# A transformer block pair in float32 on one core: two tiles of the residual left to GpSimd in three norms, silu(c) computed in pieces, and an opening that shares each tile between two blocks

## The reference

```python
def rmsnorm_2(x, g):
    xf = x.astype(jnp.float32)
    y = xf * lax.rsqrt(jnp.mean(xf * xf, axis=-1, keepdims=True) + NORM_EPS)
    return (y * g.astype(jnp.float32)).astype(x.dtype)
...
    c_act = jax.nn.silu(c)
...
        mod = c_act @ ada_w[l] + ada_b[l]
        sh_m, sc_m, g_m, sh_f, sc_f, g_f = jnp.split(mod, 6, axis=-1)
        h = modulate(rmsnorm_2(x, norm_g[l, 0]), sh_m, sc_m)
        ...
        x = x + g_m[:, None, :] * rmsnorm_2(y, norm_g[l, 1])
        h = modulate(rmsnorm_2(x, norm_g[l, 2]), sh_f, sc_f)
        y = squared_relu_mlp(h, mlp_up_w[l], mlp_down_w[l])
        x = x + g_f[:, None, :] * rmsnorm_2(y, norm_g[l, 3])
```

## Time and profile before

| what | value |
|---|---|
| time, median of 3 runs | 1792.23 us |
| lowest and highest | 1791.45 and 1792.46 us |
| the profiled execution's own time | 1791.45 us |
| its span, first to last instruction | 1789.7 us |
| TensorE busy | 1746.8 us |
| VectorE busy | 1094.8 us |
| ScalarE busy | 632.2 us |
| GpSimd busy | 95.0 us |
| mean granted TensorE clock (1 is full) | 0.993 |

### The profile page before, as it was taken

The page is one execution under the profiler, slowest core; times in us unless marked ns, Lnnn a source line. Parts: engine busy times, 40 slices in busy tenths (PEclk is TensorE's granted clock), DMA queues, the critical chain, the costliest instruction groups (busy, mean ns, idle before and its releaser), DMA issues. The chain is left out here.

```text
span 1789.7 us, 22632 instructions
## 1 busy us (share of the span) xinstructions
PE 1746.8 (98%) x8124; PEld 1413.5 (79%) x8124; DVE 1094.8 (61%) x1603; ACT 632.2 (35%) x987; POOL 95.0 (5%) x155
## 2 busy tenths in 40 slices
PE   8989999999999999999999999999999999999996
PEld 7857677888888888887888888877767788888886
DVE  6676554655555576878656565667775865434354
ACT  4226444322222353244423142425444442323231
POOL 0000000000000000100100000010000100000001
PEclk9999999999999999999999999999999999999998
DMA  6421111444444434652245555521321234333221
GB/s 230 116 85 36 48 48 56 155 148 164 146 153 153 141 106 130 219 192 83 83 176 188 203 180 203 174 85 53 118 71 38 81 97 163 105 94 95 94 82 47
DMA packets 61951, 216.63 MB, mean 121 GB/s; under 512 B 7216, under 2 KB 9392, under 8 KB 61680
## 3 DMA queue, kind: packets, MB, share of 16 engines
q1 hardware_dynamic: 45072, 154.95, 25.7%
q0 software_dynamic: 16656, 60.04, 10.9%
q10 hardware_dynamic: 144, 0.59, 0.1%
HBM read 212.67 MB, written 2.10 MB: 120 GB/s over the span
## 5 line engine op out<-in xcount | busy, mean ns | idle before, releaser
L794 ACT ACTIVATE w_hi<-w_raw 128x1024 fp32r<-128x1024 f32 x284 | 299.0, 1054 | 409.0 <-PE psum L1952 372.1
L1950 PE MATMUL psum<-h_hi,w_hi 128*128 128x512 f32 x1080 | 421.4, 390 | 2.9 <-DVE h_lo L1200 2.9
L1952 PE MATMUL psum<-h_hi,w_lo 128*128 128x512 f32 x1080 | 420.2, 389 | 0.0
L1951 PE MATMUL psum<-h_lo,w_hi 128*128 128x512 f32 x1080 | 420.2, 389 | 0.0
L1175 DVE TENSOR_TENSOR w_lo<-w_raw,w_hi 128x1024 fp32r<-128x1024 f32 x284 | 347.2, 1223 | 116.6 <-ACT w_hi L794 108.7
L1950 PE MATMUL psum<-hid_hi,w_hi 128*128 128x512 f32 x736 | 286.3, 389 | 0.0
L1951 PE MATMUL psum<-hid_lo,w_hi 128*128 128x512 f32 x736 | 286.3, 389 | 0.0
L1952 PE MATMUL psum<-hid_hi,w_lo 128*128 128x512 f32 x736 | 286.3, 389 | 0.0
L1950 PEld LDWEIGHTS psum<-h_hi,w_hi 128*128 128x128 f32 x1080 | 202.7, 188 | 46.9 <-DVE h_lo L1200 3.8
L1951 PEld LDWEIGHTS psum<-h_lo,w_hi 128*128 128x128 f32 x1080 | 202.8, 188 | 42.3 <-issue 0.5
L1952 PEld LDWEIGHTS psum<-h_hi,w_lo 128*128 128x128 f32 x1080 | 202.7, 188 | 42.2
(11 more groups left out here) (342 smaller groups left out, 1964.5 us busy)
## 6 DMA issues: line engine op xcount, KB each, us to landing
w_raw<-in_wstream SPq DMA_DIRECT2D x284, 512.0 KB, 3.6
ada_raw<-in_ada POOLq DMA_DIRECT2D x112, 512.0 KB, 3.8
x<-in_xT SPq DMA_DIRECT2D x8, 256.0 KB, 5.1
outT<-x SPq DMA_DIRECT2D x16, 128.0 KB, 1.8
con<-in_consts SPq DMA_DIRECT2D x1, 1028.0 KB, 10.1
con<-in_rope ACTq DMA_DIRECT2D x1, 576.0 KB, 5.7
w_raw<-in_wstream SPq DMA_DIRECT2D x2, 256.0 KB, 3.7
c_row<-in_crow POOLq DMA_DIRECT2D x1, 512.0 KB, 4.0
```

Of the source, the lines that this page charges most:

```text
L794: act.activation(w_hi[:, slot, :], w_raw[:, slot, :], ACT.Copy).then_inc(whi_done, 1)
L1950: pe.matmul(bank, w_hi[:, slot, w], hi[:, ra + k, :], start=k == 0, stop=False)
L1951: pe.matmul(bank, w_hi[:, slot, w], lo[:, ra + k, :], start=False, stop=False)
L1952: mm = pe.matmul(bank, w_lo[:, slot, w], hi[:, ra + k, :], start=False, stop=k == nk - 1)
```

## The change

Four edits.

1. **Opening.** Blocks 0 and 1 share each k (`kouter=2`); their first halves are loaded behind tile 0, their second halves behind tile 3, block 2 behind tile 7. 18 warm calls instead of 15.
2. **silu(c)** is done in four quarters, behind the evacuations of the gemm of five blocks; the exp stands in that gemm too.
3. **All three norms** are now of the kind with gathered sums: the `close` norm becomes inst 1, the former inst 1 becomes inst 2. `NEW_WARM` is 27 instead of 18.
4. **Tiles 6 and 7** of x: ScalarE puts the gain into y in the gemm; GpSimd multiplies by rstd and adds to x, in the stage `resum`. VectorE's `new_step` is left for tiles 0 to 5. Several steps of `resummed` read or write PSUM instead of SBUF.

```diff
-WARM_START, WARM = 15, 9
+WARM_START, WARM = 18, 9
-NEW_WARM = 18
+NEW_WARM = 27
...
-    gemm("scaled", 3, "h", h, dst="proj", dst_at=0, qscale=True)
+    gemm("scaled", 3, "h", h, dst="proj", dst_at=0, qscale=True, kouter=2)
...
-    gemm("scaled", 5, "h", h, dst="proj", dst_at=3, qscale=True)
+    gemm("scaled", 5, "h", h, dst="proj", dst_at=3, qscale=True, silu=True)
...
-    mlp(h, (0, 8, 8, 7), (8, 8, 8, 0), "g_kv", "g_m1", "r_m1")
-    close("r_f0", 21, 16, keep=True)
-    hkv = norm("hid", gain="g_kv", shift=48, splits={7: 0})
+    mlp(h, (0, 8, 8, 7), (8, 8, 8, 0), "g_kv", "g_m1", "r_m1", fore=1, old="r_f0")
+    hkv = renew("r_f0", "g_kv", 48, 1, dst="hid")
...
+        OWN = DT - 2
...
+        def root_wide(inst):
+            return psum[:, O_BANK if inst == 1 else PT_BANK, :]
...
-                if c < 2:
-                    half = slice(c * S, (c + 1) * S)
-                    sp.dma_start(w_raw[:, 0, half], wstream[0][:, half]).then_inc(raw_loaded[0] if c else raw_half, 16)
-                if c in OPEN_W:
-                    n = OPEN_W.index(c) + 1
-                    sp.dma_start(w_raw[:, n, :], wstream[n]).then_inc(raw_loaded[n], 16)
+                if c in (0, 3):
+                    half = slice(0, S) if c == 0 else slice(S, D)
+                    for n in range(2):
+                        sp.dma_start(w_raw[:, n, half], wstream[n][:, half]).then_inc(raw_loaded[n] if c else raw_half[n], 16)
+                if c == DT - 1:
+                    sp.dma_start(w_raw[:, 2, :], wstream[2]).then_inc(raw_loaded[2], 16)
...
+                if s["kind"] == "resum":
+                    pool.wait_ge(rstd_done, s["at"]["rstd"])
+                    for c in (OWN, OWN + 1):
+                        pool.wait_ge(gained_done, 2 * s["inst"] + c - OWN + 1)
+                        pool.tensor_tensor(y[:, c, :], y[:, c, :], rstd[:, :], ALU.mult).then_inc(gained_mul, 1)
+                    for c in (OWN, OWN + 1):
+                        pool.wait_ge(gained_mul, 2 * s["inst"] + c - OWN + 1)
+                        pool.tensor_tensor(x[:, c, :], x[:, c, :], y[:, c, :], ALU.add).then_inc(x_pool, 1)
...
+                    if s.get("silu") and t.b == 0:
+                        act.wait_ge(ss_done, at_["ss"])
+                        act.wait_ge(c_loaded, 16)
+                        act.activation(c_exp, c_row[:, :], ACT.Exp, scale=-1.0).then_inc(c_step, 1)
...
+                        if c >= OWN:
+                            act.wait_ge(mul_done, DT * inst + c + 1)
+                            act.activation(y[:, c, :], y[:, c, :], ACT.Copy, scale=gain_of(s["old"], c)).then_inc(gained_done, 1)
...
+                    if s["second_of"] == 2:
+                        act.wait_ge(gained_mul, 2 * s["second_of"])
+                        act.activation(rstd[:, :], resum, ACT.Exp, scale=-0.5).then_inc(root_kept, 1)
...
+            def silu_c(i):
+
+                part = slice(i * D // 4, (i + 1) * D // 4)
+                dve.wait_ge(c_step, 2 * i + 1)
+                dve.tensor_scalar(c_exp[:, part], c_exp[:, part], 1.0, None, ALU.add).then_inc(c_step, 1)
+                dve.wait_ge(c_step, 2 * i + 2)
+                dve.reciprocal(c_exp[:, part], c_exp[:, part]).then_inc(c_step, 1)
+                dve.wait_ge(c_step, 2 * i + 3)
+                dve.tensor_tensor(c_row[:, part], c_row[:, part], c_exp[:, part], ALU.mult).then_inc(c_done, 1)
...
+                        if s.get("silu") and t.b >= 1:
+                            silu_c(t.b - 1)
...
-                dve.tensor_scalar(resum, resum, 0.0, None, ALU.max).then_inc(resum_done, 1)
-                dve.wait_ge(root_done, inst + 1)
+                dve.tensor_scalar(x_mean[:, :], resum, 0.0, None, ALU.max).then_inc(resum_done, 1)
                 new_step(s, 0)
-                dve.wait_ge(held_done, DT * inst + 1)
-                dve.tensor_tensor(x[:, 0, :], x[:, 0, :], y[:, 0, :], ALU.add).then_inc(x_done, 1)
+                dve.wait_ge(held_done, OWN * inst + 1)
+                dve.tensor_tensor(x[:, 0, :], x[:, 0, :], new_val(inst, 1), ALU.add).then_inc(x_done, 1)
...
-                for c in range(DT - 2):
+                for c in range(OWN - 2):
                     val(c)
                     new_step(s, c + 2)
                     low(c)
-                val(DT - 2)
-                val(DT - 1)
-                low(DT - 2)
+                val(OWN - 2)
+                for c in range(OWN - 1, DT):
+                    val(c)
+                    low(c - 1)
                 low(DT - 1)
+                if s["inst"] == 1:
+                    dve.wait_ge(root_kept, 1)
```

More of the change, by code:

```diff
@@ L151, in renew @@
         r0 = counts["rhs"]
-        add("renew", dict(val=DT, hi=DT, rhs=DT, xup=1, xpool=DT - 1), inst=inst, old=old, gain=name, shift=shift)
+        add("renew", dict(val=DT, hi=DT, rhs=DT, xup=1, xpool=DT - 1), inst=inst, old=old, gain=name, shift=shift, dst=dst)
         return r0
-    def close(gain, middle, end, keep=False):
-        total()
-        warm(middle)
-        rstd(EPS2, wide=True)
-        update(gain)
-        warm(end)
-        rstd(EPS2, keep=keep)
     def values(group, at):
@@ L251, in make_plan, with mlp @@
     h = renew("r_m0", "g_f0", 24, 0)
-    def mlp(h, up, down, *names, ends=0):
+    def mlp(h, up, down, *names, ends=0, **last):
         for g in range(4):
@@ L289, in make_plan @@
     take("g_f1")
-    gemm("acc", 8, "h", mix, dst="y", first=True, sq=True, fore=1, old="r_m1", kouter=2, begun=6,
+    gemm("acc", 8, "h", mix, dst="y", first=True, sq=True, fore=2, old="r_m1", kouter=2, begun=6,
          turn=-counts["o"] % BANKS)
-    h = renew("r_m1", "g_f1", 88, 1)
+    h = renew("r_m1", "g_f1", 88, 2)
     hid = mlp(h, (0, 0, 0, 0), (8, 0, 0, 0), "r_f1", ends=ENDS)
@@ L307 @@
 TURN = dict(diff=2, fox=1)
-OPEN_W = (4, 7)
 SUM_AT = 6
@@ L1179, in weighted @@
             def weighted(first, upto):
+                if first == 0:
+                    dve.wait_ge(c_done, 4)
                 for u in range(first, upto):
@@ L1332, in step @@
                         dve.wait_ge(out_done, t.o + 1)
-                        dve.tensor_copy(y[:, c, :], bank).then_inc(bank_free, 1)
+                        if s["first"]:
+                            dve.tensor_copy(y[:, c, :], bank).then_inc(bank_free, 1)
+                        else:
+                            dve.tensor_tensor(y[:, c, :], y[:, c, :], bank, ALU.add).then_inc(bank_free, 1)
                         dve.wait_ge(bank_free, BANKS + t.o + 1)
@@ L1465, in new_step @@
             def new_step(s, c):
-                dve.scalar_tensor_tensor(out=y[:, c, :], in0=y[:, c, :], scalar=gain_of(s["old"], c), in1=root_wide,
+                out = y[:, c, :] if c else new_val(s["inst"], 1)
+                dve.scalar_tensor_tensor(out=out, in0=y[:, c, :], scalar=gain_of(s["old"], c), in1=root_wide(s["inst"]),
                                          op0=ALU.mult, op1=ALU.mult).then_inc(held_done, 1)
@@ L1497, in renew @@
                 at_ = s["at"]
+                hi_out, lo_out = operand(s["dst"])
                 def val(c):
@@ L1502, in val @@
                     else:
-                        dve.wait_ge(x_pool, at_["xpool"] + c)
+                        dve.wait_ge(x_pool, at_["xpool"] + (c + 2 if c < OWN else c - OWN + 1))
                     if c >= 2:
                         dve.wait_ge(rhs_ready, at_["rhs"] + c - 1)
-                    dve.scalar_tensor_tensor(out=new_val(c), in0=x[:, c, :], scalar=gain_of(s["gain"], c), in1=root_new,
+                    dve.scalar_tensor_tensor(out=new_val(s["inst"], c), in0=x[:, c, :], scalar=gain_of(s["gain"], c),
+                                             in1=root_new(s["inst"]),
                                              op0=ALU.mult, op1=ALU.mult).then_inc(val_done, 1)
@@ L1827, in _ @@
                     split_lo(s["at"]["n"] + AHEAD, (s["at"]["n"] + AHEAD) % SPLIT)
-                    if s["group"] == 1 and s["slot"] == 2:
-                        silu_c()
                     if s["slot"] == 3:
@@ L1934, in step @@
                     slot = t.n0 % SPLIT
-                    halves = at_["n"] == 0 and isinstance(t.b, int) and t.b == 0
-                    if halves:
-                        pe.wait_ge(wlo_half, 1)
-                    else:
-                        pe.wait_ge(wlo_done, t.n + 1)
+                    pe.wait_ge(wlo_done, t.n + 1)
                     for q in range(s["nout"]):
@@ L1944, in step @@
                         for k in range(nk):
-                            if halves and k == nk // 2:
-                                pe.wait_ge(wlo_done, 1)
                             if t.j == 0 and q == 0:
@@ L1969, in gemm @@
                           .then_inc(aux_done, 1)
+                    if opening and k == nk // 2:
+                        pe.wait_ge(wlo_done, len(blocks))
                     outer(s, blocks, k)
@@ L2289, in _ @@
```

(4 more changed lines are left out.)

103 lines of the change are left out of this document (54 added, 49 removed).

## The result

The changed kernel takes 1778.41 us (median of 4 runs, 1777.44 to 1779.83) against 1791.9 before: ratio 0.9925, 95% interval 0.9908 to 0.9942. The forecast was 1777.6. The profiled execution took 1778.59, its span is 1776.8, against 1789.7: 12.9 us less. Totals of one kernel scatter by 2 to 4 us from one execution to the next, so the terms are read from stages.

The account below looks back on a forecast made before the run. TensorE, busy 98% of the span, bounds the kernel. Opening 2.5, silu 8.0, norm 0 0.5, norm 1 3.2 and norm 2 0.4 sum to 14.6 us: 1776.85 for the profiled execution, median 1777.6, range 1773.5 to 1781.5.

Parts of the forecast that it names:

- Opening: First gemm: TensorE starts at about 7.55 and ends three blocks at 24.1 against 26.64, 2.5 us earlier (1.0 to 3.1).
- silu: Before the attention pairs: idle time falls from 7.4 to 0.85, 6.6 us, plus 1.4 of clock; 8.0 (6.6 to 8.4).
- The clamp: In each norm, VectorE's clamp of the mean waits for the rest of GpSimd's third operation, costing 0.75 us.
- Rival B: No collision: the clamp runs beside GpSimd, 2.2 us more gained, 1775.4; chance 0.20.
- ScalarE's copy: In the norms, the added 0.6 us copy for c=7 ends about when TensorE's sum of y squared does: costs nothing.
- Norm 0: Tiles set the pace up to k=4, then TensorE; three blocks end at 864.8 against 865.25, 0.5 us better.
- Norm 1: First tile 5.35 us earlier, part given back by slower tiles; VectorE starts the second norm at 1223.35, not 1226.42: 3.2 gained.
- Norm 2: Idle time 2.1 us with no clock fall expected; end at 1439.4 against 1439.81, 0.4 us better.
- Rival C: The clock falls in norms 0 and 2 in spite of the filler: 2.2 us less gained, 1779.8; chance 0.17.
- D: In front of the pairs another wait takes silu's place, 5 of the 8 us gone: 1782.6; chance 0.04.
- E: Little change: the opening gains nothing and silu's pieces push the weights, 1788.6 to 1795.8; chance 0.03.
- F: Norms slower: GpSimd keeps VectorE off SBUF altogether, 11.6 us a norm, 1812; chance 0.03.

Follow-up runs that it names:

- g11: The changed kernel itself, profiled and measured once more: 1778.27 us, ratio 0.9927 to the kernel before.
- f6: Changed kernel with GpSimd's add of tile 6 held until VectorE's clamp is done and tile 7's behind tiles 1 to 5: 1776.59 us, ratio 0.9917.
- e2: Kernel before with the opening edit alone: 1789.8 us, ratio 0.999.
- e3: Kernel before with the two norm edits alone (GpSimd tiles, norm 1 from gathered sums, longer filler): 1788.54 us, ratio 0.9984.
- g10: Kernel before with only the filler of its two resummed norms lengthened, 58 and 66 matmuls for 36 each: 1790.52 us, ratio 0.9994.
- f7: Changed kernel with the 20 narrow matmuls of the forget gate's sums moved behind the next block of values: 1779.63 us, ratio 0.993.
- f8: Changed kernel with f6's and f7's edits, ScalarE's copy of tile 7 behind the root's copy, fillers of 56, 62 and 62 matmuls: 1774.71 us, ratio 0.9908.
- e4: Changed kernel without its GpSimd tiles, VectorE making the steps of tiles 6 and 7 itself: 1777.17 us, ratio 0.9917.
- e1: Kernel before with the silu edit alone: 1784.88 us, ratio 0.996.
- f5: Changed kernel with the filler lengthened by each norm's idle time, 64, 70 and 74 matmuls for 54 each: 1777.09 us, ratio 0.9923.
- g9: f8 with the narrow matmuls left together as in the changed kernel: 1775.39 us, ratio 0.9911.

## Why the prediction was right, and where it wasn't

The forecast was 14.6 us in sum; the medians have 13.5 and, beside g11, 14.1. In the profiled pair it is 12.9, and the 1.7 between are 0.8 of the opening and 1.5 of norm 2, less 0.6 that silu gave on top; norms 0 and 1 came out at the size forecast. That the median came within 0.8 of 1777.6 is in part luck: the misses have different signs.

**Opening, 2.5 forecast.** The step that was short is "piece 3 at 6.1, 0.65 on ScalarE, 0.7 on VectorE, so it starts at about 7.55". In the nine executions with the new opening ScalarE gets the third piece at 6.16 to 7.18, mean 6.63, and the first matmul is 1.56 to 1.58 later, not 1.45. So the start was put 0.65 too early on the mean, with a spread of 1.0 that one trace couldn't show. In the four traces of the old order the third piece is there by 5.64 to 6.14; why it comes later in the new order stays open. In the same nine the first matmul is at 7.74 to 8.75 and the sums row at 24.18 to 25.16, mean 24.62; in the four with the old one at 26.61 to 26.87, mean 26.71. So the gain is 2.1, 1.7 in the profiled pair. In f6 the third piece is there at 6.29, and the weight load of the sums, the row at 26.64 in the earlier trace rows that I counted to, is at 24.04, against my 24.1 (its matmul, the landmark of the tables, at 24.27). Everything behind the start went as worked out: no stall at k=3 or at weight block 2. The new order saves the 2.9 us of stalls and pays with a later first matmul, since two blocks must be there.

**silu, 8.0 forecast.** The wait fell by 6.58 as said (6.6). The clock behind it was worth more than 1.4: 2.0 in the profiled pair, and 2.8 to 3.4 against e2, e3 and g10, where more of the low stretch lies behind the pairs' start (5.5 to 6.3 us at half the clock, 3.7 in before). What the prediction didn't know is the fall at 98 us, which is free while VectorE is late and costs 1.63 once it isn't. On the mean of the executions (808.95 from sums to norm 0 with the old silu, 800.13 with the new, f7 and f8 included) the edit is worth 8.8, over my upper bound of 8.4: I had taken the low stretch as one of 1.65 us and discounted it.

**The clamp, 0.75 forecast.** The collision is there, in all three norms, at 0.40 to 0.43 each. The clamp starts 0.70 us into GpSimd's third operation (832.55 - 831.85), which at 2.50/2 = 1.25 apiece had 0.55 left, not 0.75. GpSimd's pair took 2.69 in place of 2.50: its fourth operation starts at 833.1, while the clamp runs until 833.41, and takes 1.46 instead of 1.27.

```profile
L766 POOL TENSOR_TENSOR x<-x,y x2: 1266/1363/1460, 831.9 to 833.1; 128x512 f32<-128x512 f32 x2
```

Rival B (no collision) fell with the profile and with f6. The price was too high by 0.3 a norm, which outweighs the copy below.

The Trainium skill (SBUF — State Buffer, "Who interferes with whom") has such a tensor-scalar operation and GpSimd exclude each other for the whole of the one that came first. That both pay, each for the one ahead of it, and that VectorE's steps with an operand in PSUM don't, agrees with the trace. A wait for all that was left of the operation ahead, 0.55 us for the clamp and 0.3 for GpSimd, is a little over the 0.43 and 0.19 measured.

**ScalarE's copy, costed at nothing.** This step was wrong by 0.20 a norm. The copy of tile 7 ends at 827.69 in norm 0, and the logarithm of the first rstd, which used to follow TensorE's sum at once, starts at 827.95, 3.25 behind the norm's start; VectorE's first step at 4.87 where e4 and f8 have 4.67 (f8: 828.97 behind 824.30). "Ends about when" was a tie read as free.

**Norm 0, 0.5 forecast, 0.55 measured:** right in size by two errors that cancel. The old norm's three blocks end at 30.25 and 29.97 with a fall of the clock (before, e1) and at 29.34 without (e2); the new ones at 29.70 to 29.73 in all five executions. So the change removes a fall that came in two of three executions and adds 0.4 of its own. The mean gain is 0.1.

**Norm 1, 3.2 forecast, 3.18 measured**, and the same within 0.05 wherever the edit stands as it is. First matmul at 12.81 where 12.9 was given, second norm at 26.15 on VectorE and 32.75 on TensorE where 26.3 and 32.8 were: this one was right in its mechanism.

**Norm 2, 0.4 forecast, 1.13 lost.** The step that failed is "the idle time is 1.3 and 2.1 us. I expect no fall". It was 1.27 and 2.60: the head was late by 0.20 (copy), 0.42 (clamp) and 0.48 more ahead of line 1533, where VectorE's queue was idle for 0.86 and not 0.38. The clock fell in after, e3, f7 and g11, in e3 and f7 from an idle time of 2.1, and not in f5, f6 and e4 (0.36, 2.17 and 1.50). Rival C was true for this norm alone. The 0.48 is in the traces of after, g11, f5, f6 and g9 and in none of e3, e4, f7 and f8. It came again when the changed kernel was profiled a second time (g11), so it seems to go with the program and not with chance. Its cause I didn't find.

Rivals D, E and F have no support: no other wait came before the pairs, the opening and silu both gained, and VectorE's forms with one operand in PSUM run at 0.69 to 0.76 beside GpSimd in every norm.

Two versions beat both kernels: f8, 1774.71, 16.1 us under its kernel before, and g9, the same without the split, 17.0 under its own and 2.9 us under g11 on the same chip. As the split shows no gain, g9 is the simpler choice.

## What to carry to other kernels

Split a run by landmarks that stand in every version: a stage agrees to 0.1 or 0.25 us where totals scatter by 3, and it shows that a term is real, absent or masked. A filler is sized by the idle time of the place it fills, and first tried by itself in the old kernel: the same result may need no new algorithm. When a long stall is removed, what it hid comes into the time, a clock fall upstream included.

## What the runs showed of the hardware

- TensorE's clock can fall to the lower level with no idle time ahead, behind 4.7 us of narrow matmuls (8 with 8 rows, 20 with 8 columns), in six of eleven executions of the same code; it costs 1.63 us where it isn't hidden.
- Ahead of the gathered norms' first tiles it fell in three of three executions behind an idle time of 3.50 us, in four of five behind 2.6, in three of seven behind 2.1 to 2.2, and in none of twenty behind 1.7 or less.
- A VectorE clamp of 128x512 between two SBUF tiles takes 0.83 to 0.86 beside a GpSimd add (15 cases) and 0.43 alone (12 cases), and the GpSimd pair 2.69 for 2.50.
- A reciprocal of 256 columns takes 1.75 us, of 1024 columns 6.55.
- The arrival of the third piece of 256 KB in the opening differs by 1.0 us between executions of the same order (6.16 in f7, 7.18 in after).
